# Feed-forward products of 512 columns, with the two halves of each bank added outside TensorE

## What is computed

```python
def swiglu(h, w_gate, w_up, w_down):
    return (jax.nn.silu(h @ w_gate) * (h @ w_up)) @ w_down
```

## Time and profile before

| what | us |
|---|---|
| median of three runs (2224.52 to 2229.22) | 2227.09 |
| the profiled execution | 2225.59 |
| its span, first to last instruction | 2223.7 |
| feed-forward 0 and the norm ahead of it | about 206 to 399 |
| feed-forward 1 | about 538 to 732 |
| feed-forward 2 | about 865 to 1056 |
| granted clock of TensorE, mean | 0.997 |

### The profile page before, as it was taken

The page is one execution under the profiler, slowest core; times in us unless marked ns, Lnnn a source line. Parts: engine busy times, 40 slices in busy tenths (PEclk is TensorE's granted clock), DMA queues, the critical chain, the costliest instruction groups (busy, mean ns, idle before and its releaser), DMA issues.

```text
span 2223.7 us, 32058 instructions
## 1 busy us (share of the span) xinstructions
PE 2175.1 (98%) x13109; PEld 1917.1 (86%) x13123; DVE 1853.8 (83%) x2340; ACT 1336.2 (60%) x1508; POOL 84.7 (4%) x135
## 2 busy tenths in 40 slices
PE   6999999999999999999999999999999999999998
PEld 4888999889999979999798888888888888888886
DVE  7866888876998677888896988888888988888897
ACT  3574443675343776434633877777777777777775
POOL 3000111000010000010000000000000000000000
PEclk9999999999999999999999999999999999999999
DMA  9845888625877616885553999999999999999991
GB/s 369 298 184 199 334 331 300 227 76 209 300 293 279 223 39 250 309 331 184 209 200 106 369 348 368 345 371 350 354 365 345 363 347 369 345 363 355 357 364 66
DMA packets 259218, 633.33 MB, mean 285 GB/s; under 512 B 9304, under 2 KB 21625, under 8 KB 258554
## 3 DMA queue, kind: packets, MB, share of 16 engines
q1 hardware_dynamic: 234554, 536.83, 66.5%
q0 software_dynamic: 24512, 94.38, 11.2%
HBM read 630.13 MB, written 1.05 MB: 284 GB/s over the span
## 4 chain that ended last, share of the span: by engine, by line
PE 81%; DVE 12%; DMA 4%; issue 2%; ACT 1%; SPq 0%; POOL 0%; ACTq 0%; DVEq 0%
PE ps L1211 79%; DMA aring<-in_ada_rows 4%; DVE wring_rounded L2990 3%; DVE aring L3017 3%; DVE work L2990 1%; PE ps L2255 1%; PE ps L1407 1%; DVE OT L3014 1%; DVE F L2997 1%; DVE X L2997 0%; DVE F L2990 0%; PE ps L1382 0%; DVE work_rounded L2990 0%; ACT scr_rounded L2320 0%; ACT F_rounded L2320 0%
## 5 line engine op out<-in xcount | busy, mean ns | idle before, releaser
L2990 DVE TENSOR_TENSOR wring_rounded<-wring,scr_rounded 128x2048 fp32r<-128x2048 f32 (+1 forms) x314 | 568.8, 1839 | 75.8 <-ACT scr_rounded L2320 75.7
L2320 ACT ACTIVATE scr_rounded<-wring 128x2048 fp32r<-128x2048 f32 (+1 forms) x314 | 480.0, 1554 | 193.0 <-PE ps L1211 129.9
L1211 PE MATMUL ps<-wring_rounded,OT_rounded 128*128 128x512 f32 (+1 forms) x1184 | 314.7, 390 | 2.7 <-DVE wring_rounded L2990 1.7
L1211 PEld LDWEIGHTS ps<-wring_rounded,OT_rounded 128*128 128x128 f32 x1184 | 220.1, 188 | 47.2 <-DVE wring_rounded L2990 2.4
L3017 DVE CUSTOM_DVE_ANT_0 aring<-aring,F,vec 128x1024 f32<-128x1024 f32 x152 | 187.9, 1281 | 34.0 <-DMA aring<-in_ada_rows 33.2
L2990 DVE TENSOR_TENSOR wring_rounded<-wring,H_rounded 128x2048 fp32r<-128x2048 f32 (+1 forms) x85 | 193.3, 2274 | 25.5 <-ACT H_rounded L2320 25.3
L2990 DVE TENSOR_TENSOR wring_rounded<-wring,aring_rounded 128x2048 fp32r<-128x2048 f32 x84 | 192.3, 2290 | 16.1 <-ACT aring_rounded L2320 16.1
L2320 ACT ACTIVATE H_rounded<-wring 128x2048 fp32r<-128x2048 f32 (+1 forms) x85 | 162.4, 1910 | 61.0 <-issue 39.5
L2320 ACT ACTIVATE aring_rounded<-wring 128x2048 fp32r<-128x2048 f32 x84 | 161.2, 1919 | 58.1 <-PE ps L1211 58.1
L1211 PE MATMUL ps<-V_rounded,wring_rounded 128*128 128x256 f32 x1184 | 177.6, 284 | 3.8 <-DVE wring_rounded L2990 3.8
L1211 PE MATMUL ps<-work_rounded,F_rounded 128*128 128x256 f32 x1056 | 169.8, 283 | 0.0
(11 more groups left out here) (366 smaller groups left out, 3727.8 us busy)
## 6 DMA issues: line engine op xcount, KB each, us to landing
wring<-in_moe_gate SPq DMA_DIRECT2D x56, 2048.0 KB, 8.2
wring<-in_moe_up SPq DMA_DIRECT2D x56, 2048.0 KB, 8.8
wring<-in_moe_down SPq DMA_DIRECT2D x56, 2048.0 KB, 8.1
aring<-in_ada_rows POOLq DMA_DIRECT2D x88, 1024.0 KB, 8.3
wring<-in_ffn_w_gate SPq DMA_DIRECT2D x10, 2048.0 KB, 10.6
wring<-in_ffn_w_up SPq DMA_DIRECT2D x10, 2048.0 KB, 14.6
wring<-in_ffn_w_down SPq DMA_DIRECT2D x10, 2048.0 KB, 11.0
wring<-in_diff_w_in SPq DMA_DIRECT2D x6, 2048.0 KB, 16.2
```

Source lines behind the costliest of these rows:

```text
L1211: return pe.matmul(dst, lhsT, rhs, start=start, stop=stop, **kw)
L2320: return act.activation(dst, src, ACT.Copy, **kw)
L2990: return ve.tensor_tensor(dst, x, y, op)
```

## The change

The tokens' rounded part and remainder are put side by side (`HV`; `Hparts` is a view of both). One product of 512 columns multiplies a rounded weight tile with both: the left half of a bank gets rounded x rounded, the right half rounded weight x token remainder. The weight remainders are multiplied with the rounded tokens into the right half by products of 256 columns. So each half `m` of a side has a bank of its own (gate 0 and 1, up 2 and 3, the same in every group), and its value is the sum of the bank's two halves: ScalarE copies the left half into `work`, VectorE adds the right half to it. silu now reads `work`, and the product with up has both operands in `work`. Four semaphores of the sparse attention are merged into one, which moves nothing.

```diff
-                for side in sides:
-                    for m in range(2):
-                        rounded(side, m)
-                        remainder(side, m)
+                for kind, jobs, w in sides:
+                    for m, job in enumerate(jobs):
+                        job.open(pe)
+                        for k in range(KT):
+                            if m == 0 and k % 4 == 0:
+                                pe.wait_ge(ff_upper, ff_count(f, n, kind, k // 4))
+                            mm(PS[job.b][:, :], ff_buffer(kind, k // 4)[:, k % 4, m * P:(m + 1) * P], Hparts[:, :, k, :],
+                               k == 0, False)
+                        for k in range(KT):
+                            if m == 0 and k % 4 == 0:
+                                pe.wait_ge(ff_lower, ff_count(f, n, kind, k // 4))
+                            last = mm(PS[job.b][:, T:2 * T], w[:, k, m * P:(m + 1) * P], Hupper[:, k, :], False, k == KT - 1)
+                        fill(job, last)
```

```diff
                     if n >= 2:
                         act.wait_ge(ff_hid_lower, FG * f + n - 1)
-                    act.activation(ff_gated(n), PS[gate.b][:, :], ACT.Silu).then_inc(gate.bank.free, 1)
-                    if 0 < n < FG - 1:
+                    for m, job in enumerate(gate):
+                        job.filled(act)
+                        copy(ff_gated(n)[:, m * T:(m + 1) * T], PS[job.b][:, 0:T]).then_inc(ff_main, 1)
+                    if n + 1 < FG:
                         ff_split(f, L, n + 1, "g")
+                    gate[1].emptied(act)
+                    act.activation(ff_gated(n), ff_gated(n), ACT.Silu).then_inc(ff_silu, 1)
...
+                def parts_sum(n, up, jobs, dst):
+
+                    for m, job in enumerate(jobs):
+                        ve.wait_ge(ff_main, 4 * (FG * f + n) + 2 * up + m + 1)
+                        main = dst[:, m * T:(m + 1) * T]
+                        tt(main, main, PS[job.b][:, T:2 * T], ALU.add).then_inc(job.bank.free, 1)
+
                 for n in range(FG):
+                    parts_sum(n, 0, L["gj"][n], ff_gated(n))
                     if n + 1 < FG:
                         ff_lower_parts(f, L, n + 1, "g")
...
-                    gate, up = L["gj"][n], L["uj"][n]
-                    gate.emptied(ve)
-                    up.filled(ve)
-                    tt(ff_gated(n), ff_gated(n), PS[up.b][:, :], ALU.mult).then_inc(up.bank.free, 1)
+                    up = L["uj"][n]
+                    parts_sum(n, 1, up, ff_upward(n))
+                    up[1].emptied(ve)
+                    ve.wait_ge(ff_silu, FG * f + n + 1)
+                    tt(ff_gated(n), ff_gated(n), ff_upward(n), ALU.mult).then_inc(ff_product, 1)
```

More of the change, by code:

```diff
@@ L929, in build @@
         Hlower = Hlr.rearrange("p (k t) -> p k t", k=KT)
+        Hparts = HVr[:].rearrange("p s (k t) -> p s k t", k=KT)
         def ff_buffer(kind, q):
@@ L952, in ff_gated, with ff_upward @@
             return work[:, (n % 2) * 512:(n % 2 + 1) * 512]
+        def ff_upward(n):
+            return work[:, 2048 + (n % 2) * 512:2560 + (n % 2) * 512]
         def ff_hidden(n, lower):
@@ L2482, in feed_forward @@
                         beside[n]()
-                    up.filled(act)
+                    for m, job in enumerate(up):
+                        job.filled(act)
+                        copy(ff_upward(n)[:, m * T:(m + 1) * T], PS[job.b][:, 0:T]).then_inc(ff_main, 1)
                     if n + 1 < FG:
                         ff_split(f, L, n + 1, "u")
-                    up.emptied(act)
+                    act.wait_ge(ff_product, FG * f + n + 1)
                     copy(ff_hidden(n, False), ff_gated(n)).then_inc(ff_hid_upper, 1)
@@ L2492, in ff_split @@
                 if n:
-                    L[kind + "j"][n - 1].filled(act)
+                    L[kind + "j"][n - 1][1].filled(act)
                 for q in range(2):
@@ L3425, in _ @@
                 last = ve.tensor_copy(Cl[HD:P, b * T:(b + 1) * T], F[0:HD, 13 + b, :])
-            last.then_inc(ksw_ready, 1)
+            last.then_inc(compressed_made, 1)
             add_more(3)
```

89 lines of the change are left out of this document (34 added, 55 removed).

## The result

| what | before | after |
|---|---|---|
| median of four runs, us | 2226.44 (2224.52 to 2229.22) | 2256.89 (2255.15 to 2262.65) |
| span of the profiled execution | 2223.7 | 2260.9 |
| granted clock of TensorE, mean | 0.997 | 0.990 |

The change makes the kernel slower: the ratio of the times is 1.0145, with a 95% interval of 1.0133 to 1.0157. On the median that the prediction started from, 2227.09, this is 2259.4. The forecast was 2249 with a range of 2233 to 2258; 2259.4 lies above it, and the median as measured, 2256.89, just inside. The direction was right and the size was too small by 8 to 10 us.

The account below looks back on a forecast made before the run. VectorE, with loads of pieces, was taken to bound feed-forwards 0 and 1, TensorE feed-forward 2. Shifts of +9.3, +15.3 and -2.1 summed to +22.5 us, giving a forecast of 2249 us, range 2233 to 2258.

Parts of the forecast that it names:

- the mechanism: In each turn VectorE's queue grows by additions: 0.67 us ahead of the gate remainders, 0.77 at the product, 1.44 together.
- Start of a stage: In turn 0 ScalarE copies two halves ahead of the weights everyone waits for: 0.5 us for both.
- costs nothing by itself: Every group opening the same four banks was said to add no time, since banks are emptied early enough.
- The remainders stay the later ones: In the turns, up banks are emptied about 3.3 us before the up remainders are complete, so TensorE waits for remainders.
- the residual about 1.1 later: End of feed-forward 2: filter work leaves VectorE some 3 us late, the residual about 1.1 later than TensorE would.
- the forecast's -2.1: Feed-forward 2 as a whole: nine groups save 3.5 us on TensorE; with the late end, the stage is 2.1 shorter.
- granted in full (1.00) in all three stretches, and I leave it there.: TensorE's clock in all three feed-forwards was taken to stay at 1.00 after the change.
- 0.77 for each three-piece turn: In three-piece turns one pair of additions falls into a load wait, the other delays the next load: 0.77 us each.
- Additions held for their full length: Rival: each VectorE addition costs its full length, 0.3 us more in some 20 turns each, 2255; chance 0.08.
- Loads by bandwidth: Rival: loads land when bandwidth lets them, so their waits swallow both pairs of additions; +7.4, 2234.5 us; chance 0.13.
- TensorE sets the end after all: Rival: VectorE's idle time in turns 5 to 10 pays back its lag; 11.7 less, 2215.4 us; chance 0.10.
- No difference: Rival: loads absorb the additions and half of feed-forward 1's 14.0 us lag is covered; about 2228; chance 0.07.

Follow-up runs that it names:

- 1: Changed kernel, with group 0 opening and multiplying gate banks over all token tiles before opening the up banks: 2249.40 us, ratio 1.0104.
- 2: Kernel before the change, with only the wait for banks 2 and 3 added ahead of group 0 of each feed-forward: 2237.17 us, ratio 1.0051.
- Experiment 12: Changed kernel, with down weights rounded ahead of silu in the last turn of each feed-forward only: 2246.38 us, ratio 1.0094.
- 3: Changed kernel, with ScalarE rounding the down weights ahead of silu instead of behind it in every turn: 2242.38 us, ratio 1.0079.
- experiment 5: Changed kernel with gate banks first, down weights rounded ahead of silu, and VectorE's additions cut to 8 of 256 columns: 2219.98 us, ratio 0.9980.
- experiment 9: Changed kernel as it is, run and profiled a second time: 2258.12 us, ratio 1.0143.
- 6: Changed kernel with only VectorE's additions cut to 8 of their 256 columns: 2233.47 us, ratio 1.0042.
- 4: Changed kernel with gate banks first in group 0 and down weights rounded ahead of silu: 2234.66 us, ratio 1.0046.
- experiment 11: New products in feed-forward 2 alone, with gate banks first and down rounding ahead of silu; feed-forwards 0 and 1 as before: 2221.98 us, ratio 0.9989.
- 7: Changed kernel, with 11 zero products filling TensorE's wait ahead of the last down in feed-forwards 1 and 2: 2255.08 us, ratio 1.0140.
- 10: Changed kernel, with zero products filling TensorE's waits at all three stage starts and ahead of the last down of feed-forwards 1 and 2: 2254.78 us, ratio 1.0131.

## Why the prediction was too low

| part of the loss | us | by experiment |
|---|---|---|
| starts of the stages | 7.5 | 1 (11.9 alone, 2) |
| rounding behind silu, last turns | 10.5 | 12 |
| rounding behind silu, other turns | 4.0 | 3 less 12 |
| additions, cut from 256 to 8 columns | 14.7 | 5 |
| what is then left, with TensorE's saving | -4.4 | 5 |

The sum is 32.3, each row good to about 2 us; the kernel was 30.5 slower in its first runs and 32.6 in experiment 9. The rows are steps from the changed kernel to that of before, so their sum proves nothing, and they hold in this order only: with the additions cut first, that row is 23.4 and the three above it 13.5 together (experiments 5 and 6). The low clock is in these rows, beside the waits that it followed, and not a row of its own.

**Held: the mechanism.** VectorE's queue is what the change lengthens. The turn came to 19.60 us (19.57 predicted), the additions to 0.67 and 0.78 (0.67 and 0.77), and TensorE waited 2.54 us for `work_rounded` ahead of the last `down` of feed-forward 1 (2 to 3 predicted). Products of 512 columns whose tokens lie in two pieces cost what one piece costs. Two blocks of eight, 512 and 256 columns, TensorE in feed-forward 0 after the change:

```profile
275.74 2.00 PE L1217 MATMUL ps<-HV_rounded,scr_rounded 128*128 128x512 f32 x8
277.58 1.11 PE L1217 MATMUL ps<-HV_rounded,wring_rounded 128*128 128x256 f32 x8
```

The first eight took 277.58 - 275.74 = 1.84 us, 0.230 each (0.228 predicted).

**Failed: "Start of a stage", 0.5 us each.** The term looked at ScalarE's copies and not at the banks that `first_pair` opens. Measured are 2.4, 2.3 and 3.8 us in place of 0.5, and 7.5 to 11.9 us in all for a term of 1.5. The step behind it is that bank reuse "costs nothing by itself". It was not worked out for group 0, where the earlier owner of the banks is the norm. For the turns it was, with "The remainders stay the later ones", and the rows show otherwise: TensorE waits 1.5 us for a bank in four two-piece turns of feed-forward 1, and up to 2.79 in a three-piece turn of feed-forward 0 in which VectorE was late by a load (3.24 in the second profile). In the two-piece turns that costs no time by itself, since VectorE sets them and waits for nothing from TensorE; but two of the seven falls of the clock stand behind such waits in feed-forward 0. No run gives the turns other banks, so what this is worth there stays open.

**Failed: the end of feed-forward 2, "the residual about 1.1 later".** In feed-forward 1 the last turn was worked through with its 2.5 us for silu and rounding. In feed-forward 2 the same turn was settled from the room of 3.94 us, which is that of a middle turn. Its last turn has filter work ahead of the additions and no gate weights behind them. Experiment 12 puts 5.4 to 6.8 us of feed-forward 2 on the rounding behind silu in that one turn. With the start's 3.8 this is the miss of 9 to 10 us in that stage. Without both waits, experiments 4 and 11 find the forecast's -2.1: the stage was 2.2 and 2.1 us shorter, and in experiment 11 the whole kernel 2.4 faster.

**Failed: the clock, "granted in full (1.00) in all three stretches, and I leave it there."** The rows of before had shown stages in which TensorE hardly waits. The change adds waits, and 48 products behind one of them ran at 0.18 us instead of 0.12. For the waits that were filled the price in the median is the 1.8 to 3.3 us of experiments 7, 9 and 10, not settled better than that.

**Failed in part: 0.77 for each three-piece turn.** From the down remainders of turn 2 to those of turn 7 in feed-forward 0 the five turns were predicted 3.85 us longer; they were 2.3 (94.36 against 92.04), and 3.7 in the second profile. In feed-forward 1 the three turns from 5 to 8 even got shorter, 54.58 against 55.92. The kernel before is no fixed measure there. VectorE's down remainders of turns 5 and 8 in feed-forward 1, before, and in experiment 11, whose feed-forward 1 is the same code:

```profile
636.74 2.28 DVE L2990 TENSOR_TENSOR wring_rounded<-wring,F_rounded 128x2048 fp32r<-128x2048 f32 x1
...
692.66 2.29 DVE L2990 TENSOR_TENSOR wring_rounded<-wring,F_rounded 128x2048 fp32r<-128x2048 f32 x1
```

```profile
636.54 2.29 DVE L3066 TENSOR_TENSOR wring_rounded<-wring,F_rounded 128x2048 fp32r<-128x2048 f32 x1
...
690.76 2.29 DVE L3066 TENSOR_TENSOR wring_rounded<-wring,F_rounded 128x2048 fp32r<-128x2048 f32 x1
```

55.92 us in one execution and 54.22 in the other, a difference of 1.7 us between two executions of the same code, and the sum had taken one execution's load waits to a tenth. The error of this term ran the other way and hid the 2.3 us of feed-forward 1's start. So the good figure for that stage is in part luck: two errors that cancel.

**The rivals.** *Additions held for their full length* falls: they start 0.33 apart (592.62 to the end of both is 0.74, of which 0.41 is the last one's own). The rule that stood beside it, of the Trainium skill, page "VectorE: DVE Perf Modes", section "The DRAIN you can't avoid", would have given 2255, near the measured time, for a reason that the rows do not show. *Loads by bandwidth* had a part in feed-forward 1, as just said, but not its price. *TensorE sets the end after all* needed VectorE less than 3 us late in turn 10, and there VectorE waited another 2.50 us for `F_rounded`, in all three stages. With small additions and both waits away (experiment 5) the time does fall under that of before, but by 4.4 us and not by 11.7. *No difference* falls by the measured ratio, 1.0133 at the least.

## What to carry over

When a change lets a loop's first pass touch more buffers than before, ask of each one who owned it last before the loop, and not only who owns it inside. Work the last pass of every stage through by itself: what covered a wait in a middle pass can be missing there. The rounding behind silu cost 10.5 us in three last turns and 4.0 in thirty others. An edit that saves the busiest engine 0.39 us a turn and loads the second busiest with 1.45 is worth making only in the stages where a turn has room for it; made in feed-forward 2 alone, with both new waits taken out, it gained 2.4 us.

## What the runs showed of the hardware

- In the first profile of the changed kernel TensorE's granted clock fell to 0.50, its level of 1.2 GHz, behind waits of 1.9 to 2.8 us and stayed there for some 3.5 to 7 us, in which 256-column products started up to 0.25 us apart in place of 0.12. The same wait was followed by a fall in one execution and not in the next (2.40 us at the end of feed-forward 0, experiment 9).
- A GpSimd product of 128 x 512 with two SBUF operands took 2.19 us beside VectorE's subtractions, and two of these took 3.45 us in place of 2.35. VectorE lost 1.10 us and was spared 0.61.
- A pair of VectorE additions of 8 columns still takes 0.15 us ahead of an instruction that does not wait for it and 0.27 ahead of one that does, against 0.67 and 0.78 for 256 columns (experiments 5 and 6, the changed kernel).
